# Feed-forward up projections: one 512-column matmul for the high and low activations, and another start address for both

## The reference, cut to what matters

```python
x = x + jnp.square(jax.nn.relu(h2 @ w_up[l])) @ w_down[l]          # 1024 -> 4096 -> 1024
...
def swiglu(h, w_gu, w_down):                                       # 1024 -> 2 x 2816 -> 1024, four times
    g, u = jnp.split(h @ w_gu, 2, axis=-1)
    return (jax.nn.silu(g) * u) @ w_down
```

## Time and profile before

| | |
|---|---|
| median of 3 runs | 1453.48 us (1450.79 to 1454.17) |
| the profiled execution | 1449.68 us |
| its span, first to last instruction | 1447.9 us |
| busy: PE matmuls / weight loads / DVE / ACT / GpSimd | 1393.1 / 1350.0 / 915.3 / 723.5 / 192.2 us |
| granted TensorE clock, mean | 0.99 of full speed (2.4 GHz) |

### The profile page before, as it was taken

The page is one execution under the profiler, slowest core; times in us unless marked ns, Lnnn a source line. Parts: engine busy times, 40 slices in busy tenths (PEclk is TensorE's granted clock), DMA queues, the critical chain, the costliest instruction groups (busy, mean ns, idle before and its releaser), DMA issues.

```text
span 1447.9 us, 28167 instructions
## 1 busy us (share of the span) xinstructions
PE 1393.1 (96%) x11538; PEld 1350.0 (93%) x11538; DVE 915.3 (63%) x1317; ACT 723.5 (50%) x1149; POOL 192.2 (13%) x210
## 2 busy tenths in 40 slices
PE   5889899999999999999999999999999998999998
PEld 5777789999999999998899999999999987999998
DVE  7998776666545655547766565556565467656554
ACT  7722745544434544446447444445454474544443
POOL 0465000022100111004201111011110010111100
PEclk9999899999999999999999999999999999999999
DMA  9233324555554545553434555544555441355551
GB/s 372 102 115 108 139 88 141 186 198 176 202 185 172 198 176 213 179 202 135 158 120 148 189 186 194 199 175 175 185 207 181 169 173 59 120 190 185 194 199 59
DMA packets 36814, 244.33 MB, mean 169 GB/s; under 512 B 4208, under 2 KB 5360, under 8 KB 8816
## 3 DMA queue, kind: packets, MB, share of 16 engines
q1 hardware_dynamic: 34992, 238.17, 45.4%
q10 hardware_dynamic: 1728, 4.81, 0.9%
HBM read 241.67 MB, written 1.05 MB: 168 GB/s over the span
## 4 chain that ended last, share of the span: by engine, by line
PE 84%; DVE 9%; ACT 4%; issue 2%; DMA 1%; DVEq 0%; ACTq 0%
PE ps L1906 50%; PE ps L1948 27%; DVE wlo L1094 3%; PE ps L2144 1%; PE ps L2170 1%; ACT whi L599 1%; PE ps L2160 1%; ACT ahi L853 1%; ACT pP L789 1%; PE ps L1964 1%; PE ps L2049 1%; DVE zz L1279 1%; DVE pP L1385 0%; DVE t L1241 0%; DVE t L1240 0%
## 5 line engine op out<-in xcount | busy, mean ns | idle before, releaser
L1094 DVE TENSOR_TENSOR wlo<-raw,whi 128x1024 fp32r<-128x1024 f32 (+1 forms) x434 | 505.7, 1207 | 256.2 <-ACT whi L599 256.0
L1906 PE MATMUL ps<-ahi,whi 128*128 128x256 f32 x2112 | 598.9, 284 | 21.8 <-DVE wlo L1094 17.5
L599 ACT ACTIVATE whi<-raw 128x1024 fp32r<-128x1024 f32 (+1 forms) x434 | 427.7, 1034 | 348.5 <-PE ps L1948 178.9
L1906 PE MATMUL ps<-alo,whi 128*128 128x256 f32 x2112 | 591.9, 280 | 0.0
L1906 PE MATMUL ps<-ahi,wlo 128*128 128x256 f32 x2112 | 591.1, 280 | 0.0
L1906 PEld LDWEIGHTS ps<-ahi,whi 128*128 128x128 f32 x2112 | 398.6, 189 | 29.1 <-DVE wlo L1094 13.0
L1906 PEld LDWEIGHTS ps<-alo,whi 128*128 128x128 f32 x2112 | 397.9, 188 | 0.7 <-issue 0.7
L1906 PEld LDWEIGHTS ps<-ahi,wlo 128*128 128x128 f32 x2112 | 398.1, 189 | 0.0
L1842 POOL TENSOR_TENSOR hlo<-fh,hhi 128x256 f32 (+3 forms) x104 | 85.8, 825 | 747.4 <-ACT hhi L909 534.5
L1550 DVE TENSOR_TENSOR fa<-ps,r 128x512 f32<-128x512 f32 x104 | 72.0, 692 | 173.8 <-PE ps L1906 173.6
L1948 PE MATMUL ps<-whi,hhi 128*128 128x256 f32 x960 | 149.5, 276 | 0.0
(11 more groups left out here) (350 smaller groups left out, 1346.8 us busy)
## 6 DMA issues: line engine op xcount, KB each, us to landing
raw<-in_w_gu SPq DMA_DIRECT2D x88, 1024.0 KB, 4.8
raw<-in_w_fd SPq DMA_DIRECT2D x44, 1024.0 KB, 4.8
raw<-in_w_up SPq DMA_DIRECT2D x16, 1024.0 KB, 4.8
raw<-in_w_dn SPq DMA_DIRECT2D x16, 1024.0 KB, 4.8
raw<-in_w_ret SPq DMA_DIRECT2D x13, 1024.0 KB, 4.8
raw<-in_w_mg SPq DMA_DIRECT2D x8, 1024.0 KB, 4.9
raw<-in_w_o SPq DMA_DIRECT2D x8, 1024.0 KB, 5.8
raw<-in_w_mem SPq DMA_DIRECT2D x4, 1024.0 KB, 4.8
```

What stands on the lines that cost most here:

```text
L599: nc.scalar.activation(whi[:, m % SPL, c], raw[:, n % RAW, c], ACT.Copy).then_inc(S("w_hi"), 1)
L1094: ins = tt(wlo[:, m % SPL, c], raw[:, n % RAW, c], whi[:, m % SPL, c].bitcast(F32), ALU.subtract)
L1906: ins = mm(dst, lhsT, rhs, start=k == 0 and p == 0, stop=k == kt - 1 and p == len(pairs) - 1)
```

## The change: what it does

1. `ahi` and `alo` become the two halves of one tensor `act2`, so that one matmul can move `ahi[k]` and `alo[k]` side by side: 512 columns over the same `whi` piece, into a whole PSUM bank, the high sum in the left half and the low sum in the right. The `wlo` matmul with 256 columns adds to the left half. An up unit of an FFN is now 16 matmuls of 512 columns and 16 of 256 (`ffn_unit`). Its two tiles c need two banks, g%2 and 4+g%2.
2. The two halves of a bank have to be added. ACT copies the right half to SBUF (`fl`, `low_sum`), DVE adds the left half to it (`fa`), then multiplies by `r`; for each c apart. `evac` comes after the second. PE signals `ffn_left` after c = 0.
3. ACT's order in a unit is now: copy of c = 0, high part of the unit before (`high`), weight split, Silu, copy of c = 1.
4. Banks 4 and 5 belong to `down` as well, so its first unit waits, before its second 128 tokens, for `evac` of the last up unit.
5. `st` moves ahead of `act2`. Worked out as above, `ahi` and `alo` now start at 0 modulo 128, like the weights. `hhi` and `hlo` stay at 64.
6. A few semaphores are merged; their waits stay.

```diff
-        ahi = sb("ahi", [P, KT, T], F32R)
-        at_alo = [base[0]]
-        alo = sb("alo", [P, KT, T], F32R)
         st = sb("st", [P, TT, 8])
+        act2 = sb("act2", [P, 2, KT, T], F32R)
+        ahi, alo = act2[:, 0], act2[:, 1]
...
+        def ffn_banks(g):
+
+            return two(g % 2), two(4 + g % 2)
...
+                def low_sum(i, u, c):
+                    if c:
+                        sem, v = done(up + u)
+                        act.wait_ge(sem, at_round(v, i, RAW))
+                    else:
+                        act.wait_ge(S("ffn_left"), at_round(h0 + u + 1, i, RAW))
+                    nc.scalar.activation(fl[:, u % 2, c], ffn_banks(g0 + u)[c][:, 1], ACT.Copy).then_inc(S("low_sum"), 1)
...
+                    else:
+                        low_sum(i, u, 0)
+                        high(i, u - 1)
+                        weights(up + u, i, UNIT)
+                    if kind == "gu":
+                        act.wait_ge(S("joined"), at_round(3 * (h0 + u) + 2, i, 3 * RAW))
+                        nc.scalar.activation(fs[:, b], fa[:, b, 0:T], ACT.Silu).then_inc(S("silu"), 1)
+                    if not opening:
+                        low_sum(i, u, 1)
...
-                    tt(fab, two((g0 + u) % 2), over(r[:, 0:T], 2), ALU.mult).then_inc(S("evac"), 1)
-                    if i is not None or u:
-                        weights(up + u, i, UNIT)
+                    for c, bank in enumerate(ffn_banks(g0 + u)):
+                        if c and not opening:
+                            weights(up + u, i, UNIT)
+                        dve.wait_ge(S("low_sum"), at_round(2 * (h0 + u) + c + 1, i, 2 * RAW))
+                        tt(fab[:, c], bank[:, 0], fl[:, b, c], ALU.add).then_inc(S("joined"), 1)
+                        dve.wait_ge(S("joined"), at_round(3 * (h0 + u) + 2 * c + 1, i, 3 * RAW))
+                        tt(fab[:, c], fab[:, c], r[:, 0:T], ALU.mult).then_inc(S("evac" if c else "joined"), 1)
...
+            def ffn_unit(n, i=None, need=None, halfway=None):
+
+                g = GROUP[n]
+                pe.wait_ge(S("evac"), at_round(g - 1, i, RAW))
+                pe.wait_ge(S("w_lo"), at_round(SPLIT_BEFORE[n] + 1, i, RAW))
+                for c, bank in enumerate(ffn_banks(g)):
+                    if halfway and c:
+                        halfway()
+                    for k in range(KT):
+                        if need and c == 0:
+                            need(k)
+                        ws = slice(k * 2 * P + c * P, k * 2 * P + c * P + P)
+                        mm(bank, whi[:, n_slot(n), ws], act2[:, :, k], start=k == 0, stop=k == KT - 1, skip_group_check=True)
+                        ins = mm(bank[:, 0], wlo[:, n_slot(n), ws], ahi[:, k], start=False, stop=k == KT - 1,
+                                 skip_group_check=True)
+                    ins.then_inc(S("unit_split_done" if c else "ffn_left"), 1)
...
                 down((1, 2, 4, 5, 7)[f], dn, ndn, hhi, hlo,
-                     lambda u: pe.wait_ge(S("hid_lo"), h0 + (u + 1) * nup // ndn))
+                     lambda u: pe.wait_ge(S("hid_lo"), h0 + (u + 1) * nup // ndn),
+                     between={(0, 1): lambda: pe.wait_ge(S("evac"), GROUP[dn])})
```

51 lines of the change are left out of this document (28 added, 23 removed).

## The result

The changed kernel takes **1466.11 us** (median of 4 runs, 1464.50 to 1472.72), the kernel before 1452.87 us (median of 4): ratio **1.0097**, 95% interval 1.0066 to 1.0127. It is slower by about 13 us, where 1444 (1432 to 1459) was predicted. A second set of runs (e14) gave 1.0120 (1.0085 to 1.0155), 20 us between the medians. The profiled execution of after is the slowest of its four: 1472.72 us, span 1470.9.

What follows compares the result with a forecast made beforehand. PE, busy 96% of the span, was taken to bound the kernel, so the distance between matmul starts counts. The terms -23 - 3 + 10 + 2 + 5 = -9 us gave 1444 us, range 1432 to 1459.

Steps and rivals of the forecast that it cites:

- Part 1: Up-unit matmuls in the gated FFNs: a step falls from 353 to 336 ns, 23 us saved.
- narrow 120: Up units: the 256-column matmul over `wlo` takes 120 ns at the new remainder, set by the next load.
- rival C: Up steps: each weight load takes 8 to 11 ns from the stream; 342 to 347 ns, 1453 to 1461 us; chance 0.24.
- Part 2: Longer chain behind each up unit: hides under PE in gated FFNs; first FFN at 5.51 us a unit, 3 us saved.
- the ring: ACT and DVE cycle per up unit: split, add, multiply, `fh`, `hhi`, next split; in the first FFN `hhi` ends at D+5.65.
- Part 3: First down unit of each FFN: PE waits 1.8 us for the last `evac`, longer in the first FFN; 10 us lost.
- Part 4: Opening of each FFN: first `evac` comes later after four DVE steps; 0.4 us on each, 2 us lost.
- Part 5: Units outside the FFN up units: the new remainder moves matmuls from 117.7 or 113.3 to 120 ns; 5 us lost.

Runs made afterwards that it cites:

- e14: The changed kernel run once more, unchanged; ratio 1.0120 to the kernel before.
- m1: TensorE alone: three forms of the up step and the down form at several addresses; the 512-column float32r matmul is followed after 228 to 237 ns.
- m2: TensorE alone: rows of 32 matmuls varying moving columns, stationary columns and data type; 512 float32r columns with 32 stationary ones take 231 ns, bfloat16 216.
- e6: The changed kernel with each 512-column matmul issued as two of 256, the rest of the change kept; 1475.2 us.
- e1: The kernel before with only both split activations moved from 64 to 0 bytes modulo 128; 1462.0 us, ratio 1.0073.
- e4: The kernel of e3 with the first FFN alone back in the form of the kernel before; 1453.3 us, ratio 1.0021.
- e3: The changed kernel with the second half of each up unit in banks 6 and 7 instead of 4 and 5; 1452.9 us, ratio 1.0041.
- e12: The kernel before with an extra lead matmul of 288 columns ahead of each down stage and another inside each up stage; 1448.7 us, ratio 0.9993.
- e9: The kernel of e7 with one extra matmul of 256 to 384 columns ahead of each down stage; 1452.4 us, ratio 1.0012.
- e7: The kernel of e4 with both activations at 32 bytes modulo 128 instead of 0; 1452.8 us.
- e11: The kernel of e7 with one extra matmul of 288 columns ahead of each of the five down stages; 1452.3 us, ratio 1.0020.
- e2: The changed kernel with both activations put back to 64 bytes modulo 128, weights at 0; 1469.1 us.
- e8: The kernel before with both split activations at 32 bytes modulo 128 and nothing else changed; 1466.8 us.

## Why the prediction was wrong, by its steps

**Part 1 failed, and it is the step that decides.** The prediction put it as "512 columns over `whi`: 216 ns, the load of the next weights hidden" and read the excess of the 256-column rows as the load's. m1 has the wide matmul at 228 to 237 ns on average with PE alone, m2 has it at 231 with a quarter of the load and at 216 only in bfloat16. What takes the room is the float32r stream itself. The rows that were used, plain float32 ones, were of another kind: they have two passes, 429 ns for 512 columns, and their 216 says nothing of float32r. The narrow 120 was right. The step measures 351 ns instead of 336, 2 saved where 17 were forecast. Of the time, 1.7 us a gated stage are the wide form's at equal addresses (e6 against after), and 0.9 us of the remainder (e1) are to be taken off: 3.2 us saved in the four, where 23 stood. What the text said would speak for rival C, "224 or more after the wide one", is what came; C's sign was right, its ranges of 342 to 347 ns and of 1453 to 1461 us ended too low, and its mechanism (each load takes its part) is not it.

The Trainium skill ("TensorE: Matmul & The Clock Gate", Back-to-back issue gap) gives columns/2.4 + 2.5 ns for a warm matmul. The trace of m2 agrees with it for bfloat16 (109.1 and 215.8) and not for float32r (232 to 234 at 512 columns).

**Part 2** held for the gated FFNs: e6 and e1 have the same 126.36 us with the new evacuation and the old. For the first FFN it was mis-sized: 5.51 us a unit were forecast, 6.1 came, +5.0 us instead of -3. e4 shows that the new form there costs 96.50 - 92.16 = 4.3 us, and e6 that it is the evacuations and not the matmuls. The lines above show where the ring was mis-sized. The split that runs beside GpSimd's `hlo` takes 2.75 us where 2.36 were taken. And two hand-overs take 0.13 us where 0.03 were taken from a gated unit: the multiply ends at 344.78 and `fh` begins at 344.91, it ends at 345.60 and `hhi` begins at 345.73. The earlier trace rows had 0.14 for the second. Together 0.59 us, which is 6.10 less 5.51. No experiment took the overlap with GpSimd away, so that part is read and not shown.

The Trainium skill ("SBUF — State Buffer", SBUF: two separate sides) has a port pair that either a DVE instruction with two SBUF inputs or a GpSimd one holds for its whole length while the other waits. The rows agree in that only overlapped splits are long: in after the 385 without an overlap take at most 1.23 us for one half, those with one 1.54 on average and up to 2.30.

**Part 3** was right in its mechanism: 10 us forecast, 9.7 measured as waits, and e3 took them away. The five down stages grew by more, 5.1 + 4 x 1.96 = 12.9 us: from start to start PE loses some 0.3 us more than the idle time in its record (1.95 us where the record has 1.67), and the prediction left out what followed a stand of 3 us, 1.7 us more at the lower clock.

**Part 4**, 2 us for the openings, was not there: in the gated FFNs the up stages of e6 and e1 include them and are equal.

**Part 5** had the sign and over three times the size, 5 us where 1.4 came. `w_out` lost 1.0 us of the forecast 2.6, `w_ret` and the other token units of the retention 0.4 (20.35 to 20.78 us), and the up form goes from 117.8 to 118.6 ns and not to 120. What it could not know is that the paces mix: 117.8 is one of two at 64, and 118.6 an average in which 115 and 122 occur.

The sum with these: -3.2 (gated up) + 5.0 (first FFN) + 5.1 (its down stage, wait and clock) + 4 x 1.96 (gated seams) + 1.4 (token units) = +16.1 us for the profiled stages, where the medians have 13.2 in the first set of runs and 20.2 in e14. The 23 us between the two profiled spans hold besides one slow down stage (2.2) and 7 us of clock before the first FFN (290.6 us against 283.6 in e14). The stretch between the fourth FFN and the fifth gives 3.1 us back (92.9 us against 96.0), in which the granted clock was 1.00 in after and 0.91 to 0.97 in before. For e3 the same terms give 5.0 - 3.2 + 1.4 + 0.4 = +3.6 us; measured 3.4 between the medians (1452.91 against 1449.49), 5.9 by the ratio.

No version is faster than the kernel before clear of the noise. The nearest, e12 and e9, are not to be told from it. e7 and e11 contain a real gain, 2.3 and 2.2 us in each gated up stage, and lose it to slow down stages; the one profiled execution of e11, with three of the five fast, took 1445.1 us.

## What to carry to other kernels

Price a matmul from a row of its own data type: a float32r stream cost 0.45 ns a column from 256 columns up, and joining two matmuls of 256 into one of 512 saved 4.7 ns a step with the activations at 0 (e6 against after), nothing at 64 (e2), and 5 or 9 at 32 (e8 with 352 or 356 ns a step, e7 with 347). Before a second PSUM bank is added to a stage, look which of the next stage's tiles uses that bank; here another choice of banks took 8 us off the time without touching anything else. Where equal instructions run at two paces, compare stage by stage, since one slow down stage costs 2.3 or 3.4 us, and the matmuls of the four gated FFNs together won 3.2.
